# Attention stages of a three-layer block: who halves, what signals a load, in which order the products stand, and where the grouped scores lie

## The reference

```
na:   s = q @ k_window.T * 64**-0.5 + rpb,  q @ k_ctx.T * 64**-0.5   (8x16 window of a 16x64 grid, 256 context keys)
gqa:  s = q @ k.T * 64**-0.5                (1,024 keys and 256 context keys; 4 query heads share one k, v)
fox:  s = q @ k.T with a forget gate, causal (1,024 keys)
p = softmax(s, axis=-1);  o = p @ v
```

## Time and profile before

| | |
|---|---|
| Median of 3 runs | 5924.98 us (5895.28 to 5936.32) |
| The profiled execution | 5909.1 us, span 5907.3 us |
| Busy | PE 4519.5 (77%), PEld 3823.1 (65%), DVE 2372.5 (40%), ACT 1496.2 (25%), POOL 743.4 (13%) |
| Granted TensorE clock, mean | 0.869 |
| na, first transposes to last product | 705.59 to 1037.7 us |
| gqa, second scores to last product | 1063.57 to 1437.5 us |
| fox, first scores to last normalize | 4572.89 to 4794.57 us |

### The profile page before, as it was taken

One profiled execution on the slowest core, in us unless ns is written; L12 is line 12 of the kernel. 1 busy time (PEld: TensorE's weight loads), 2 busy tenths in 40 slices (PEclk: granted clock), 3 DMA queues, 4 the chain that ended last, 5 costly groups with the idle time before them and its releaser, 6 DMA issues. The chain is left out here.

```text
span 5907.3 us, 68257 instructions
## 1 busy us (share of the span) xinstructions
PE 4519.5 (77%) x25392; PEld 3823.1 (65%) x25392; DVE 2372.5 (40%) x4130; ACT 1496.2 (25%) x3014; POOL 743.4 (13%) x734
## 2 busy tenths in 40 slices
PE   7996378787899934999999105997794846899993
PEld 2995367686699913999999102444793635688783
DVE  3112455233511155777677335455311434211232
ACT  2111244454411133222222101002311433221222
POOL 0000122000000024444344241000000000000000
PEclk9997589898999956999899556998896977999996
DMA  6222431201322254111111432023222113111113
GB/s 256 89 92 76 117 62 39 50 14 67 107 89 78 80 230 152 33 37 39 39 39 29 103 147 93 22 82 118 95 83 77 35 49 111 61 46 49 39 62 116
DMA packets 316283, 472.73 MB, mean 80 GB/s; under 512 B 109459, under 2 KB 240627, under 8 KB 311480
## 3 DMA queue, kind: packets, MB, share of 16 engines
q1 hardware_dynamic: 315748, 464.38, 24.5%
q10 hardware_dynamic: 288, 5.07, 0.2%
HBM read 341.16 MB, written 133.20 MB: 80 GB/s over the span
## 5 line engine op out<-in xcount | busy, mean ns | idle before, releaser
L497 PE MATMUL g_acc<-g_wh,l_x_high 128*128 128x416 f32 (+2 forms) x1856 | 635.4, 342 | 56.8 <-DVE g_wl L53 56.8
L497 PE MATMUL g_acc<-g_wh,l_x_low 128*128 128x416 f32 (+2 forms) x1856 | 637.6, 344 | 0.0
L497 PE MATMUL g_acc<-g_wl,l_x_high 128*128 128x416 f32 (+2 forms) x1856 | 633.8, 341 | 0.0
L497 PEld LDWEIGHTS g_acc<-g_wh,l_x_high 128*128 128x128 f32 x1856 | 351.4, 189 | 63.4 <-DVE g_wl L53 59.5
L1583 POOL TENSOR_TENSOR scan_X<-scan_GA,scan_masks 64x256 f32<-64x256 f32 x480 | 361.7, 754 | 240.5 <-ACT scan_GA L1511 205.9
L548 DVE COPY g_o<-g_acc 128x416 f32<-128x416 f32 (+2 forms) x116 | 65.4, 564 | 726.1 <-PE g_acc L497 726.1
L497 PEld LDWEIGHTS g_acc<-g_wl,l_x_high 128*128 128x128 f32 x1856 | 351.5, 189 | 5.8
L497 PEld LDWEIGHTS g_acc<-g_wh,l_x_low 128*128 128x128 f32 x1856 | 350.8, 189 | 3.5
L2863 PE MATMUL ffi_acc<-l4a_x_high,ffi_wh 128*128 128x512 f32 x704 | 274.8, 390 | 12.9 <-DVE ffi_wl L53 12.9
L535 ACT COPY g_o<-g_acc 128x416 f32<-128x416 f32 (+2 forms) x116 | 56.4, 486 | 878.6 <-PE g_acc L497 878.6
L2863 PE MATMUL ffi_acc<-l4a_x_low,ffi_wh 128*128 128x512 f32 x704 | 274.6, 390 | 0.0
(11 more groups left out here) (483 smaller groups left out, 9886.5 us busy)
## 6 DMA issues: line engine op xcount, KB each, us to landing
scan_F<-s_FE SPq DMA_DIRECT2D x160, 192.0 KB, 3.7
s_U<-g_o SPq DMA_DIRECT2D x120, 208.0 KB, 1.9
feat_u<-s_U SPq DMA_DIRECT2D x30, 832.0 KB, 11.1
s_FE<-feat_f SPq DMA_DIRECT2D x10, 2304.0 KB, 7.9
ffi_w<-in_w_ffn_in SPq DMA_DIRECT2D x44, 512.0 KB, 3.7
conv_u<-s_U SPq DMA_DIRECT2D x24, 768.0 KB, 7.9
g_w<-in_attn_w_in SPq DMA_DIRECT2D x8, 1664.0 KB, 6.9
pj_o<-s_O SPq DMA_DIRECT2D x26, 512.0 KB, 4.4
```

The source lines that it names most:

```text
L497: mm = pe.matmul(acc[r][:, 0:wn], xT[x][:, k, m * P:(m + 1) * P], v[b][:, k, :], start=(k == 0 and n == 0), stop=(k == kt - 1 and n == 2))
```

## The change

- GpSimd does the whole of the halving in na and gqa: for a head that brings new k, `k_high` by a copy, `k_low` by a subtraction; then q's high copy and low subtraction; then, in na, the five biases. ScalarE's `halve` is gone. The first maximum of a head waits for its own bias alone.
- `k_loaded` and `v_loaded` take the place of `kv_loaded`. The halving (fox: the scores) waits for k alone, the first products of a head for v. SP issues k before it waits for `summed`; only v (and in na the tables, which stand behind it) is issued after.
- na and fox: TensorE's list is transposes of w-2, scores of w, products of w-2.
- gqa (`shared`): two scores buffers of 1,280 columns over five banks. The middle bank holds the last 256 columns of one and the first 256 of the other. A unit's scores in its own banks are written one unit ahead; the two matmuls of 256 columns in the shared bank ("late") wait for the exponential of the unit before. TensorE's list is, for each w: late scores of w, transposes of w-1 (first two groups), own scores of w+1, transposes of w-1 (third group), products of w-1. `pt` goes from 3 banks to 2 and `po` from 2 to 1.

```diff
-def attention_stage(nc, name, ident, K, nk, units, heads, kv_of, q_in, k_in, v_in, o_out, LA, split, table_in=None, window=None, causal=None):
+def attention_stage(nc, name, ident, K, nk, units, heads, kv_of, q_in, k_in, v_in, o_out, LA, shared, split, table_in=None, window=None, causal=None):
...
-    NS = LA
-    NPT = 8 - NB * NS - 2
+    NPT = 2
+    HALF = 512 * NB - 256 if shared else 512 * NB
+    NPO = 1 if shared else 2
...
-        scores = [st.ps(f"scores{i}", [P, 512 * NB]) for i in range(NS)]
+        both = st.ps("scores", [P, 2 * HALF])
+        scores = [both[:, i * HALF:(i + 1) * HALF] for i in range(2)]
         pt = [st.ps(f"pt{i}") for i in range(NPT)]
-        po = [st.ps(f"po{i}") for i in range(2)]
...
+        def at0(w):
+            return 256 if shared and w % 2 and width(w) < HALF else 0
+
+        def parts(w):
+            out, at = [], at0(w)
+            for c0, n in units[work[w][1]]["keys"]:
+                while n:
+                    m = min(n, 512 - (at + w % 2 * HALF) % 512)
+                    out.append((at, c0, m))
+                    at, c0, n = at + m, c0 + m, n - m
+            mine = [p for p in out if shared and (p[0] + w % 2 * HALF) // 512 == NB - 1]
+            return [p for p in out if p not in mine], mine
...
                         if g >= 2:
-                            sp.wait_ge(summed, lead[g - 1] * NU)
                             if split:
                                 sp.wait_ge(k_high_out, g - 1)
                                 sp.wait_ge(k_low_out, g - 1)
+                            else:
+                                sp.wait_ge(scored, lead[g - 1] * NU)
                         for r in range(2 if split else 1):
-                            sp.dma_start(k_raw[g % 2][r * HD:r * HD + K, :], k_in(kv_of[h])).then_inc(kv_loaded[g % 2], 16)
-                        sp.dma_start(v[g % 2][:, :, :], v_in(kv_of[h])).then_inc(kv_loaded[g % 2], 16)
+                            sp.dma_start(k_raw[g % 2][r * HD:r * HD + K, :], k_in(kv_of[h])).then_inc(k_loaded[g % 2], 16)
+                        if g >= 2:
+                            sp.wait_ge(summed, lead[g - 1] * NU)
+                        sp.dma_start(v[g % 2][:, :, :], v_in(kv_of[h])).then_inc(v_loaded[g % 2], 16)
...
             @block.gpsimd
             def _(pool):
                 for h in range(heads if split else 0):
-                    g = halves(pool, h)
+                    g = kv(h)
                     if h:
-                        pool.wait_ge(k_low_out, kv(h - 1) + 1)
+                        pool.wait_ge(q_low_out, h)
                         if window is not None:
                             pool.wait_ge(bias_ready, 5 * h)
+                    if lead[g] == h:
+                        pool.wait_ge(k_loaded[g % 2], QN * (g // 2 + 1))
+                        if g >= 2:
+                            pool.wait_ge(scored, lead[g - 1] * NU)
+                        high(pool, k_high[g % 2][:, :], k_raw[g % 2][:, :]).then_inc(k_high_out, 1)
+                        pool.wait_ge(k_high_out, g + 1)
+                        low(pool, k_low[g % 2][:, :], k_raw[g % 2][:, :], k_high[g % 2][:, :]).then_inc(k_low_out, 1)
+                    pool.wait_ge(k_low_out, g + 1)
+                    pool.wait_ge(loaded[h % 2], QN * (h // 2 + 1))
+                    if h >= 2:
+                        pool.wait_ge(scored, (h - 1) * NU)
+                    high(pool, q_two[h % 2][:, :], q_raw[h % 2][:, :]).then_inc(q_high_out, 1)
                     pool.wait_ge(q_high_out, h + 1)
                     low(pool, q_two[h % 2][HD:P, :], q_raw[h % 2][HD:P, :], q_two[h % 2][HD:P, :]).then_inc(q_low_out, 1)
-                    pool.wait_ge(q_low_out, h + 1)
-                    if lead[g] == h:
-                        pool.wait_ge(k_high_out, g + 1)
-                        if g >= 2:
-                            pool.wait_ge(scored, lead[g - 1] * NU)
-                        low(pool, k_low[g % 2][:, :], k_raw[g % 2][:, :], k_high[g % 2][:, :]).then_inc(k_low_out, 1)
                     if window is not None:
+                        pool.wait_ge(q_low_out, h + 1)
                         if h == 0:
                             pool.wait_ge(const_in, 16)
                         pool.wait_ge(table_loaded[h % 2], 32 * (h // 2 + 1))
...
-                def score(w):
+                def score(w, late=0):
...
+                            pe.wait_ge(k_loaded[g % 2], QN * (g // 2 + 1))
+                    if shared and late:
+                        if w:
+                            scores_done(pe, w - 1)
+                    elif w >= 2:
+                        scores_done(pe, w - 2)
+                    pieces = parts(w)[late]
...
+                    if late or not parts(w)[1]:
+                        mm.then_inc(scored, 1)
+
+                def turning(w, some):
+                    if 0 in some:
+                        pe.wait_ge(probs, w + 1)
                     for i, tl in enumerate(groups[w]):
                         n = first[w] + i
+                        if i not in some:
+                            continue
                         if n >= NPT:
                             pe.wait_ge(turned, n - NPT + 1)
                         for a, t in enumerate(tl):
                             mm = pe.transpose(pt[n % NPT][:, a * P:(a + 1) * P], prob[w % 2][:, t * P:(t + 1) * P], ident[:, :])
                         mm.then_inc(trans, 1)
...
-                    if w >= 2:
-                        pe.wait_ge(normed, w - 1)
+
+                def mix(w):
+                    h, x = work[w]
+                    u, g = units[x], kv(h)
+                    if x == 0:
+                        pe.wait_ge(v_loaded[g % 2], 16 * (g // 2 + 1))
+                    if w >= NPO:
+                        pe.wait_ge(normed, w - NPO + 1)
                     for i, tl in enumerate(groups[w]):
                         pe.wait_ge(turned, first[w] + i + 1)
                         for t in tl:
-                            mm = pe.matmul(po[w % 2][:, 0:HD], probT[w % 2][:, t, :], v[g % 2][:, u["tiles"][t], :],
+                            mm = pe.matmul(po[w % NPO][:, 0:HD], probT[w % 2][:, t, :], v[g % 2][:, u["tiles"][t], :],
                                            start=(t == 0), stop=(t == len(u["tiles"]) - 1))
                     mm.then_inc(summed, 1)
 
-                for w in range(N + LA):
-                    if w < N:
-                        score(w)
-                    if w >= LA:
-                        mix(w - LA)
+                if shared:
+                    score(0)
+                    score(1)
+                    if parts(0)[1]:
+                        score(0, 1)
+                    for w in range(1, N + 1):
+                        if w < N and parts(w)[1]:
+                            score(w, 1)
+                        turning(w - 1, (0, 1))
+                        if w + 1 < N:
+                            score(w + 1)
+                        turning(w - 1, (2,))
+                        mix(w - 1)
+                else:
+                    for w in range(N + LA):
+                        if w >= LA:
+                            turning(w - LA, (0, 1))
+                        if w < N:
+                            score(w)
+                        if w >= LA:
+                            mix(w - LA)
...
-                def halve(h):
-                    g = halves(act, h)
-                    nc.scalar.copy(q_two[h % 2][:, :], q_raw[h % 2][:, :]).then_inc(q_high_out, 1)
-                    if lead[g] == h:
-                        act.wait_ge(kv_loaded[g % 2], KN * (g // 2 + 1))
-                        nc.scalar.copy(k_high[g % 2][:, :], k_raw[g % 2][:, :]).then_inc(k_high_out, 1)
...
-                    n = width(w)
+                    n, a = width(w), at0(w)
                     act.wait_ge(maxed, w + 1)
...
-                    src = biased[w % 2] if has_bias(w) else scores[w % NS]
-                    nc.scalar.activation(prob[w % 2][:, 0:n], src[:, 0:n], ACT.Exp, bias=mx[:, w % 2:w % 2 + 1],
+                    src = biased[w % 2] if has_bias(w) else scores[w % 2]
+                    nc.scalar.activation(prob[w % 2][:, 0:n], src[:, a:a + n], ACT.Exp, bias=mx[:, w % 2:w % 2 + 1],
...
-                if split:
-                    halve(0)
-                    halve(1)
                 for w in range(N + LA):
                     if w >= LA:
                         turn(w - LA)
-                        if split and work[w - LA][1] == 0 and 2 <= work[w - LA][0] + 1 < heads:
-                            halve(work[w - LA][0] + 1)
                     if 0 <= w - LA + 1 < N:
...
-                    u, n, src = units[x], width(w), scores[w % NS]
+                    u, n, a, src = units[x], width(w), at0(w), scores[w % 2]
...
-                        dve.wait_ge(bias_ready, 5 * (h + 1))
+                        dve.wait_ge(bias_ready, 5 * h + u["bias"] + 1)
...
```

(46 more changed lines are left out.)

7 lines of the change are left out of this document (4 added, 3 removed).

## The result

The changed kernel took 5,729.26 us (median of 4 runs, 5,727.43 to 5,729.7), the kernel before 5,921.65 (4 runs beside it): a ratio of 0.968, interval 0.965 to 0.971. The profiled execution took 5,729.1 us.

What follows compares the result with a forecast made beforehand. TensorE was taken to bound the attention stages, waiting for the first copy before products and at na's heads. Gains of 88 (na), 41 (gqa) and 40 (fox), together 169 us, took the median from 5,925.0 to 5,756; range 5,715 to 5,815.

Steps and rivals of the forecast that it cites:

- The covered gap in na: Wide units of na: scores fill the 0.70 us idle between transposes and products; period falls from 3.89 to 3.19 us.
- Rival (b): na and gqa: another wait replaces the gap, periods stay 3.89 and 4.89, 69 us not won: 5,825; chance 0.12.
- ScalarE's ring: Wide units of na: transposes to copy, copies, exponential to the next transposes; together 3.01 us, below the period of 3.19.
- The stall: Heads of na: TensorE's 6.18 us wait behind ScalarE's cast of k, plus 3.0 of slow clock, 9.2 in all, goes.
- The chain of loads and halving: Heads of na: q and k land early, tables last; biases ready at 13 us, at worst 20, of a 30 us head.
- Rival (c): Heads of na: tables or v come late, so 6.2 and 3.0 us stay at six or seven heads: 5,816; chance 0.08.
- Rival (d): na: slow copies make GpSimd the bound, slower than before; 30 us a copy gives 6,077 or so; chance 0.03.
- The turn: Change of head in na: after two short iterations TensorE needs 4.9 us against 3.2 of work, so 1.7 us idle.
- Rival (a): Turns of na and gqa: TensorE could fall to 1.2 GHz at all 15; 32 us more, 5,788; chance 0.15.
- 2.28 to the end of the maximum, 1.2 to the transposes: Change of head in na: the last two parts of the 4.9 us from transposes to the new unit's transposes.
- the term of the gaps: fox: gaps before the products, 54 us at most, are covered except 14 at the first units of heads: 40 less.
- more is won than I count: Whole kernel: the starting and turning costs kept in the forecast shrink, so the gain is larger; chance 0.07.

Runs made afterwards that it cites:

- Order only: The kernel before, with transposes ahead of the scores in na and fox, all else as before: 5,820.36 us, ratio 0.984.
- gqa with one buffer: The changed kernel, with gqa back to one buffer of scores and its old order (scores, transposes, products of one unit): 5,751.31 us, ratio 0.972.
- the narrow units apart: The changed kernel, with na's two narrow units of a head behind its third and sixth wide unit instead of together at its end: 5,723.22 us, ratio 0.967.
- halves only: The changed kernel with TensorE's list and gqa's buffers as before, keeping GpSimd's halving, separate k and v signals and the wait for the own bias: 5,831.18 us, ratio 0.987.

## Why the prediction was right

**The gaps.** The covered gap in na was to give a period of 3.19; it is 3.10. In gqa 4.51 were predicted and 4.52 measured, turn 1.8 and 1.63, head 40.0 and 40.1. Order only, and gqa with one buffer, show the order as the cause and price it: 44.5 in na, 51.5 in fox, 31 in gqa (there together with the buffers that it needs). Rival (b), ScalarE's ring in place of the gap, is out: the periods are TensorE's own lists, with 0.2 to 0.3 us to spare for the ring.

**The stall.** It is gone, with its slow clock. The chain of loads and halving was read rightly: the biases of a head are done at 774, 13 us into the head from 761 to 793, as predicted, and the tables land in 9.6 us at worst. Rival (c) is out. The prediction didn't separate the signal from the move. The kernels with the casts back on ScalarE and with k and v together do: either removes the wait for v, and the move alone suffices. SP's earlier issue of k stands in both.

**GpSimd.** The copy was the one cost without a row. I took 2.2 us between 0.43 and 2.9; it is 1.25. The estimate of 1.07 worked out from the Trainium skill (GPSIMD Engine Reference, When to use GPSIMD), whose rule is line rate for one-input operations, was nearer than my scaling with the columns. That sizes the head at 16 us on GpSimd instead of 18, and nothing hung on it: with 7.7 us more a head na is no longer. Rival (d) was a real mechanism at the wrong distance. It measured GpSimd by the old head of 43.8 us; the new one is 29.9, and at 16 and 24 us a head GpSimd hides, at 39 it sets the pace. Its sum of 6,077 also takes off na's 88 where the 81 of gqa and fox were meant, a slip of 7.

**The turn.** 1.7 us was predicted, 2.27 is measured. The term that failed is "2.28 to the end of the maximum, 1.2 to the transposes": the exponential also waits for the normalize of w-2, which stands behind that maximum on VectorE. With that wait taken away the idle time is 1.80. The same miss made me count the narrow units apart too cheaply.

**The slow clock.** Rival (a) happened in part. At three of seven turns of na the clock fell to a mean of 0.64, and such a head is 1.5 to 1.8 us longer (31.4 to 31.7, and 29.9): 5.0 us, where 3 were counted. In gqa I had kept 10 us for it; the clock was 0.99 over 321 us, a loss of about 3 at its start, and it didn't fall at a turn. The Trainium skill (TensorE: Matmul & The Clock Gate, Part 1) has activity lift the clock. The trace agrees at the turns of na: with 2.27 us of idle time the clock fell at three of seven, with 1.80 at two of seven in both kernels that have it, with two of 0.70 a head at none.

The clock is also a good part of the gain, and the prediction counted on it only at the stalls of na. The length of each window times what its mean clock falls short of 1.00 is the time that the slow clock can have cost at most: 37, 19 and 9 us before, 10, 3 and 3 after. By this estimate up to 48 of the 192 us are slow clock that went with the waits.

**The sizes.** Predicted 88, 41 and 40; measured 90.5, 48.6 and 52.6. In gqa the surplus is the slow clock that I kept, some 7 of the 10 us. Its start cost 4 (second scores 24.1 us behind the first load, where 20.2 were needed), where 2 to 3 were counted. In fox the term of the gaps was not what failed:

```profile
PEld fox_po L878 <- issue: 13.6, 41, 0.6
PEld fox_po L878 <- DVE fox_o L964: 4.8, 8, 0.8
PEld fox_pt L865 <- ACT fox_prob L913: 4.6, 14, 1.4
```

The waits before the products, all causes together, were 54.5 us (46.0 of them in the earlier trace rows) and are 18.9: 36, where 40 were forecast. The rest I had left out. Waits before the transposes fell from 11.0 to 4.6. The first head went from 32.11 to 21.66, when the others went from 26.71 to 20.77, so 4.5 more came off there, at a stage's clock of 0.96 before and 0.98 after. The first transposes come 1.6 us sooner behind the first load. That makes some 48 of 52.6. The remaining 4 or 5 weren't tested; they may be what na shows, where seven transposes followed by a stop cost 0.86 to the next instruction, and 0.77 followed by scores: 0.09 a unit, 6 us over 64 units.

So the case of "more is won than I count" is what happened on top of the forecast: in gqa the cost I had kept for the slow clock was smaller than its bound, and in fox the order removed more than the gaps before the products. That na came out within 3 us is in part luck: its turns (0.57 us too low, seven times) and its slow clock (2 too low) were made up for by a period 0.09 below the forecast, 64 times.

## What to carry to other kernels

Where a matmul waits for a copy of its own operands, put independent work of the next unit between them, and check that the next ring (maximum, exponential) still fits: in gqa with one buffer the reorder cost 67 us (376.6 to 443.2), with two overlapping buffers it won 31. Count every semaphore in front of the instruction that decides a turn; a buffer of two columns of sums cost 4 to 5 us in na. Before you credit a small difference, see how much the same code varies, and in which part. When two edits remove the same wait, try each without the other before crediting either.

## What was not expected of the hardware

The clock's loss doesn't go by the length of an idle time alone. One of 0.70 a unit in na and 0.38 in gqa ran at full clock before the change; 0.99 a unit of 5.5 lowered it again and again and brought gqa to a clock of 0.90; 2.27 once a head of na lowered it at every second turn. The turn of gqa had an idle time of 1.72 in the kernel before and in halves only: the clock fell at five of seven in the one and at one of seven in the other. The fp32 to fp32r cast of 128x1280 takes 1.25 us on GpSimd and 1.27 on ScalarE: for this operation GpSimd is no slower. The subtraction of 64x1280 takes 2.88 to 2.92 us on GpSimd, as long as that of 128x1280, and 1.49 on VectorE:

```profile
950.37 1.49 DVE L53 TENSOR_TENSOR gqa_q_two<-gqa_q_raw,gqa_q_two 64x1280 fp32r<-64x1280 f32 x1 [12.60 <-ACT gqa_q_two L929]
```
